# Neighbourhood attention of one layer in blocks of grid columns: 256 grid keys a block, scores in six one-bank places of PSUM

## The reference, cut to what matters

```python
def _neighbourhood_attention(q, k, v, kc, vc, rpb, scale):
    rows = length // GRID_W                      # 512 // 64 = 8
    wr = min(NA_ROWS, rows)                      # 8
    col = jnp.arange(GRID_W, dtype=jnp.int32)
    col_start = jnp.clip(col - NA_COLS // 2, 0, GRID_W - NA_COLS)      # NA_COLS = 16
    col_idx = col_start[:, None] + jnp.arange(NA_COLS, dtype=jnp.int32)[None, :]
    col_bias = rpb[:, :, col_idx - col[:, None] + (NA_COLS - 1)].astype(jnp.float32)
    ...
        s_nb = jnp.einsum('bhqd,bhrqkd->bhqrk', q_row, k_win).astype(jnp.float32) * scale + bias[None]
        s_ctx = jnp.einsum('bhqd,bhcd->bhqc', q_row, kc).astype(jnp.float32) * scale
        p = jax.nn.softmax(jnp.concatenate([s_nb.reshape(b, h, GRID_W, n_nb), s_ctx], axis=-1), axis=-1)
        ...
        return (jnp.einsum('bhqrk,bhrqkd->bhqd', p_nb, v_win)
                + jnp.einsum('bhqc,bhcd->bhqd', p[..., n_nb:], vc))
```

## Time and profile before

| | |
|---|---|
| median of 3 runs | 3726.51 us (3724.79 to 3728.86) |
| span of the profiled execution | 3722.8 us |
| the profiled execution's own time | not listed apart from its span; the median stands 3.7 us above it |
| PE busy | 3442.9 us, 92% of the span |
| DVE, ACT, POOL busy | 2015.8, 1320.7, 418.9 us |
| granted TensorE clock, mean | 0.972 |
| instructions | 47620 |
| near stage, first near scores to first matmul of `w_out` | 2116.77 to 2239.20 us of the span |

### The profile page before, as it was taken

How to read it: one execution, slowest core, us unless ns; L and a number is a source line. 1 busy time by engine, 2 the same in 40 slices (tenths; PEclk the granted TensorE clock), 3 DMA queues, 4 the chain that set the end, 5 groups by cost and what they waited for, 6 DMA issues and landing times. The chain is left out here.

```text
span 3722.8 us, 47620 instructions
## 1 busy us (share of the span) xinstructions
PE 3442.9 (92%) x19041; PEld 2781.6 (75%) x19041; DVE 2015.8 (54%) x3218; ACT 1320.7 (35%) x2013; POOL 418.9 (11%) x355
## 2 busy tenths in 40 slices
PE   6997889999989878999999878999999889989998
PEld 5885678888878656787787547888888666668886
DVE  3555556635546555868623764564554455555344
ACT  4224433212223354323222563531221644544233
POOL 2002440000000040000001570000000013300000
PEclk8997999999999999999999999999999999999999
DMA  5440033434422103555421002244343121113332
GB/s 184 124 124 24 1 90 104 132 99 125 125 68 68 46 1 97 164 158 171 131 71 40 11 21 61 76 127 122 101 128 89 47 45 31 33 57 97 96 104 72
DMA packets 466714, 322.59 MB, mean 87 GB/s; under 512 B 51408, under 2 KB 439262, under 8 KB 466496
## 3 DMA queue, kind: packets, MB, share of 16 engines
q1 hardware_dynamic: 456864, 299.93, 26.9%
q0 software_dynamic: 9632, 19.62, 1.9%
HBM read 312.94 MB, written 4.55 MB: 85 GB/s over the span
## 5 line engine op out<-in xcount | busy, mean ns | idle before, releaser
L1018 PE MATMUL PS<-HH,SPH 128*128 128x512 f32 (+1 forms) x3424 | 1180.2, 358 | 77.8 <-ACT HH L1781 20.7
L1018 PE MATMUL PS<-HL,SPH 128*128 128x512 f32 (+1 forms) x3424 | 1136.6, 355 | 4.8 <-DVE HL L2324 4.8
L1018 PEld LDWEIGHTS PS<-HH,SPH 128*128 128x128 f32 x3424 | 655.4, 191 | 194.9 <-issue 67.6
L1018 PE MATMUL PS<-HH,SPL 128*128 128x512 f32 (+1 forms) x3424 | 744.0, 357 | 0.0
L1018 PEld LDWEIGHTS PS<-HL,SPH 128*128 128x128 f32 x3424 | 646.3, 191 | 94.9 <-DVE HL L2324 7.7
L2207 DVE TENSOR_TENSOR SPL<-RAW,SPH 128x1024 fp32r<-128x1024 f32 (+3 forms) x367 | 458.1, 1248 | 389.5 <-ACT SPH L1647 388.8
L1018 PEld LDWEIGHTS PS<-HH,SPL 128*128 128x128 f32 x3424 | 582.8, 191 | 96.2 <-issue 5.3
L1647 ACT ACTIVATE SPH<-RAW 128x1024 fp32r<-128x1024 f32 (+3 forms) x367 | 393.9, 1074 | 720.3 <-PE PS L1018 464.5
L1018 PE MATMUL PS<-MH,SPH 128*128 128x512 f32 (+1 forms) x1056 | 361.8, 356 | 4.0 <-ACT SPH L1647 4.0
L1018 PE MATMUL PS<-ML,SPH 128*128 128x512 f32 (+1 forms) x1056 | 359.6, 355 | 0.0
L2521 DVE SCALAR_TENSOR_TENSOR X<-PS,MOD,X 128x512 f32<-128x512 f32 (+1 forms) x144 | 95.3, 662 | 403.1 <-PE PS L1018 401.2
(11 more groups left out here) (343 smaller groups left out, 3530.0 us busy)
## 6 DMA issues: line engine op xcount, KB each, us to landing
MS<-in_mod_turned SPq DMA_DIRECT2D x144, 512.0 KB, 3.4
RAW<-in_l_w_up SPq DMA_DIRECT2D x88, 512.0 KB, 3.8
RAW<-in_w_gate SPq DMA_DIRECT2D x44, 512.0 KB, 4.6
RAW<-in_w_val SPq DMA_DIRECT2D x44, 512.0 KB, 4.5
RAW<-in_w_down SPq DMA_DIRECT2D x32, 704.0 KB, 5.8
RAW<-in_l_w_down SPq DMA_DIRECT2D x32, 704.0 KB, 5.6
RAW<-in_w_in SPq DMA_DIRECT2D x40, 512.0 KB, 4.9
MS<-in_w_mod SPq DMA_DIRECT2D x32, 512.0 KB, 4.6
```

The costliest lines, as they stand in the source:

```text
L1018: return pe.matmul(o, a, b, start=start, stop=stop)
```

## The change

- **Layout.** `w_in`'s tiles of neighbourhood queries, keys and values are written to SBUF by grid columns: queries in four blocks u of 8 rows by 16 columns (columns 8-23, 24-39, 40-55, and 0-7 with 56-63), keys and values in four blocks of 8 rows by 16 columns. A query block needs only two key blocks, 256 keys. ACT's copy of a tile becomes three instructions for queries, two for keys and values.
- **Near steps** have 256 grid keys and 256 context keys: `nj` is 4 in place of 6. So 4 matmuls of 256 columns for scores, 8 transposes in two rounds, and an "o" of 4 matmuls over 256 queries (context) and 8 over 128 (grid).
- **PSUM.** A near side takes 512 columns, one bank, so that the three tiles hold six; the wait is for the exp of the side that last used the place.
- **Maxima, exp.** The custom instruction handles 256 columns and writes back to PSUM, one exp of 512 columns reads PSUM, and the addition of two sums is gone.
- **POOL** multiplies 512 columns a side and no longer loads biases.
- **The bias table** is half as large: 4 fills and 109 transfers of 1 to 16 columns. `load_bias` is 32 transfers of 16 partitions x 4 x 128, on SP's queue, all four pairs between the loads of `w_out`'s second and third tile.
- **Output.** The high and the low part of a near "o" are two instructions of 128 columns each, back in row order.

```diff
+NEAR = 256
...
-        BIAS = [[place(f"BIAS{r}{i}", [P, 14 * 64], F32, at0 + i * 3584) for i in range(2)]
+        BIAS = [[place(f"BIAS{r}{i}", [P, 4 * NEAR], F32, at0 + i * 16 * NEAR) for i in range(2)]
                 for r, at0 in enumerate((e0, big0 + 2 * TOK * 4))]
...
-        biasd = nc.dram_tensor("bias_rows", (64, 120 * 64), F32, kind="Internal").ap()
+        biasd = nc.dram_tensor("bias_rows", (64, 120 * 32), F32, kind="Internal").ap()
...
+        def query_cols(u):
+            return list(range(16 * u + 8, 16 * u + 24)) if u < 3 else [*range(8), *range(56, 64)]
+        def grid_block(x, u):
+            g = x.rearrange("p (r c) -> p r c", c=GRID_W)
+            if u < 3:
+                return g[:, :, 16 * u + 8:16 * u + 24]
+            return g.rearrange("p r (g k) -> p r g k", k=8)[:, :, 0:8:7, :]
+        def by_columns(x, c):
+            if 6 <= c < 10:
+                inner = x[:, 0:LAT].rearrange("p (r c) -> p r c", c=GRID_W)[:, :, 8:56]
+                return [(slice(0, 384), inner.rearrange("p r (u c) -> p u r c", u=3)),
+                        (slice(384, LAT), grid_block(x[:, 0:LAT], 3)), (slice(LAT, TOK), x[:, LAT:TOK])]
+            return [(slice(0, LAT), x[:, 0:LAT].rearrange("p (r u c) -> p u r c", u=4, c=16)), (slice(LAT, TOK), x[:, LAT:TOK])]
+        def near_keys(x, u):
+            if u < 3:
+                return x[:, P * u:P * u + NEAR]
+            return x.rearrange("p (b n) -> p b n", n=P)[:, 0:4:3, :]
+        def near_values(u, k):
+            return u + k if u < 3 else 3 * k
...
+            def place(self, n, e):
+                k = 2 * n + e
+                near = self.steps[n][0]["kind"] == "near"
+                return k % 3, 512 * (k // 3 % 2) if near else 0, 512 if near or self.steps[n][0]["nq"] < LAT else TOK
+            def place_free(self, n, e):
+                bank, a, m = self.place(n, e)
+                for k in range(2 * n + e - 1, -1, -1):
+                    other, b, w = self.place(k // 2, k % 2)
+                    if other == bank and b < a + m and a < b + w:
+                        return self.side(k // 2, k % 2) + 1
+                return self.sides_begin() if self.base["steps"] else 0
...
+            def out_parts(self, n, x, c):
+                G, blocks = self.steps[n]
+                if G["kind"] == "near":
+                    return [(slice(P * (u % 2), P * (u % 2) + P), grid_block(x[:, c, 0:LAT], u)) for u in (blocks[-1] - 1, blocks[-1])]
+                return [(slice(0, 256), x[:, c, self.out_cols(n)])]
...
+            def load_bias(p):
+                slots = biasd.rearrange("(u i) (b r n) -> i u b (r n)", u=4, b=2, n=16)
+                for e in range(2):
+                    for r in range(8):
+                        r0 = (2 * p + e) * 15 + 7 - r
+                        dst = BIAS[p % 2][e][16 * r:16 * r + 16, :].rearrange("p (u b n) -> p u b n", u=4, b=2)
+                        for b in range(2):
+                            sp.dma_start(dst[:, :, b, :], slots[:, :, b, r0 * 16:r0 * 16 + P]).then_inc(S.bias_landed[p % 2], 16)
+            def load_biases(A):
+                sp.wait_ge(S.bias_made, 16 * 109)
+                load_bias(0)
+                near = [n for n, (G, _) in enumerate(A.steps) if G["kind"] == "near"]
+                sp.wait_ge(S.s_done, A.side(near[0], 1) + 1)
+                load_bias(1)
+                for p in (2, 3):
+                    sp.wait_ge(S.bias_free, 8 * (p - 1))
+                    load_bias(p)
...
+                        if x is L["w_out"] and li == 2 and j == 2:
+                            load_biases(L["attention"])
...
-            def load_bias(p):
-                for e in range(2):
-                    for half in range(2):
-                        r0 = (2 * p + e) * 15 + (1 - half)
-                        pool.dma_start(BIAS[p % 2][e][64 * half:64 * half + 64, :], biasd[:, r0 * 64:(r0 + 14) * 64])\
-                            .then_inc(S.bias_landed[p % 2], 16)
...
-                    if G["kind"] == "near" and blocks == [0] and G["pair"] < 3:
-                        if G["pair"]:
-                            pool.wait_ge(S.bias_free, 8 * G["pair"])
-                        load_bias(G["pair"] + 1)
...
-                for k in range(8):
+                for k in range(4):
                     pool.dma_start(biasd.rearrange("c (a n) -> (c a) n", a=2)[:, k * 480:(k + 1) * 480], MASK[:]).then_inc(S.bias_filled, 16)
-                pool.wait_ge(S.bias_filled, 128)
+                pool.wait_ge(S.bias_filled, 64)
                 rpb = d["l0_rpb_2"].rearrange("h r c -> (h r) c")
-                flat = biasd.rearrange("c (r k) -> c r k", k=64)
-                for c in range(64):
+                flat = biasd.rearrange("c (b r k) -> c b r k", b=2, k=16)
+                for row in range(64):
+                    u, c = row // 16, query_cols(row // 16)[row % 16]
                     start = min(max(c - 8, 0), 48)
-                    pool.dma_start(flat[c, :, start:start + 16], rpb[:, start - c + 15:start - c + 31]).then_inc(S.bias_made, 16)
+                    split = 16 - start % 16
+                    block = start // 16 - u if u < 3 else start // 48
+                    for b, a, n, k in ((block, 16 - split, split, 0), (block + 1, 0, 16 - split, split)):
+                        if n:
+                            pool.dma_start(flat[row, b, :, a:a + n], rpb[:, start - c + 15 + k:start - c + 15 + k + n],
+                                           allow_slow_non_contiguous=n == 1).then_inc(S.bias_made, 16)
...
-                    ring = 2 if A.mla else 3
                     at = G["q0"] + blocks[0] * P
                     for e in range(2):
-                        if part == 0 and A.side(n, e) >= ring:
-                            pe.wait_ge(S.exp_done, A.side(n, e) - ring + 1)
...
+                            k, p0, _ = A.place(n, e)
+                            ps = PS[k]
                             nk = G["nj"] * P
-                            if nk == TOK:
+                            if G["kind"] == "near":
+                                a = NEAR * part
+                                keys = kt[rows, LAT:TOK] if part else near_keys(kt[rows, 0:LAT], blocks[0])
+                                last = mm(ps[:, p0 + a:p0 + a + NEAR], qt[rows, at:at + P], keys, True, True)
...
+                        for j in (2, 3):
+                            for e, rows in enumerate(G["rows"]):
+                                mm(turn_bank(r)[rows, 0:256], G["v"][e](LAT // P + j - 2), PTR[:, NTC * e + j, at:at + 256], j == 2, False)
+                        for u in (blocks[-1] - 1, blocks[-1]):
+                            a = P * (u % 2)
+                            for j in range(2):
+                                for e, rows in enumerate(G["rows"]):
+                                    last = mm(turn_bank(r)[rows, a:a + P], G["v"][e](near_values(u, j)), PTR[:, NTC * e + j, at + a:at + a + P],
+                                              False, j == 1 and u == blocks[-1])
+                        last.then_inc(S.t_done, 1)
+                        return
...
-                        if G["kind"] == "near":
-                            act.activation(ex[:, 0:LAT], ex[:, 0:LAT], ACT.Exp, bias=top, accum_out=total)
-                            last = act.activation(ex[:, LAT:TOK], ps[:, LAT:TOK], ACT.Exp, bias=top, accum_out=ctx_sum(n, e))
-                        else:
-                            last = act.activation(ex, ps, ACT.Exp, bias=top, accum_out=total)
+                        last = act.activation(ex, ps, ACT.Exp, bias=top, accum_out=total)
...
+                        if c < 6:
+                            act.activation(big(c), LIN[s % 2][:, 0:TOK], ACT.Copy).then_inc(S.tile_free, w.one(S.tile_free, t + 1))
+                        else:
+                            dst = VRAW[:, c - 14, :] if c >= 14 else big(c)
+                            for cols, src in by_columns(LIN[s % 2][:, 0:TOK], c):
+                                last = act.activation(shaped(dst[:, cols], src), src, ACT.Copy, scale=0.125 if 10 <= c < 14 else 1.0)
...
-                            if A.slot_turned(n, e):
-                                dve.wait_ge(S.t_done, A.slot_turned(n, e))
-                            ex, ps = A.probs(n, e), A.scores(n, e)
-                            b = BIAS[G["pair"] % 2][e][:, (6 - 2 * u) * 64:(6 - 2 * u) * 64 + LAT]
+                            ps = A.scores(n, e)
+                            b = BIAS[G["pair"] % 2][e][:, NEAR * u:NEAR * u + NEAR]
                             ctx_top, all_top = ATT[:, 32 + e:33 + e], ATT[:, 34 + e:35 + e]
-                            dve.tensor_reduce(ctx_top, ps[:, LAT:TOK], AX.X, ALU.max).then_inc(S.dve_step, w.one(S.dve_step))
+                            dve.tensor_reduce(ctx_top, ps[:, NEAR:2 * NEAR], AX.X, ALU.max).then_inc(S.dve_step, w.one(S.dve_step))
                             dve.wait_ge(*w.last)
```

(6 more changed lines are left out.)

53 lines of the change are left out of this document (31 added, 22 removed).

## The result

The changed kernel took 3705.69 us, the median of 4 runs (3702.32 to 3708.89); the kernel before took 3727.36 beside them. The ratio is 0.9942, 95% interval 0.9928 to 0.9956, or 22 us less. Measured again with 5 runs (experiment e1) it was 3703.15 us and 0.9932 (0.9918 to 0.9946), 25 us less. Forecast were 3701.5 us and 25.0 less.

A forecast was written before the change was run, and what follows sets the result against it. The near stage was taken as bound by hand-overs between engines running fixed lists; 25.2 us saved there less 0.2 for `w_in`'s last copy, 25.0 off 3726.5, gave 3701.5 us, range 3694 to 3716.

The forecast's parts named there:

- The sum: Near stage: 4.1 us saved in the first pair, 6.6 in each of three, 1.3 at the end, 25.2 us in all.
- The five intervals: Between score matmuls of one pair in the near stage: 5.5, 2.2, 5.9, 4.8 and 2.6 us, sum 21.0, before 27.64.
- fifth interval: Context scores in a pair: PE's own 1.07 + 0.57 + 0.57 and 0.4 for POOL or an exp, 2.6 us (4.47 before).
- last copy of `w_in`: ACT's copy before the first scores becomes three instructions: 0.2 us more, bounds 0.1 and 0.5.
- POOL's list for the table: 109 transfers for 64 and 4 fills less: about 24 us more issuing, no term, as POOL then idles until 1087.
- wait for exp: PE's 0.96 us wait in the second interval goes, as the place three sides back is another bank.
- DVE's lateness: Third interval: the "o" waits about 1.0 us for its bank, giving back the saving; 5.9 us (5.92 before).
- Small pieces cost as much as large ones: Rival, chance 0.12: narrow matmuls, custom instruction, POOL and "o" parts keep large prices, 15 us back, 3716 us.
- The bias queue binds: Rivals on SP's bias issues: mildly, from 0.66 us an issue, 3720 us (0.06); hard, from 0.92, 3769 us (0.04).
- The fourth interval: With the context step's short "o" in a pair: 4.8 us (5.91 before), including 0.3 wait for the high part.
- shortens an engine that is not late: Said of ACT: one exp of 512 columns, below 0.72 us, in place of 1.17 us for two.
- sign of being wrong: Pairs over 23 us apart, a reduce waiting for the bias, or time moving outside of 2019 to 2240 us.

The follow-up runs named there:

- e3: Changed kernel with the six PSUM places undone, near sides in a three-tile ring again: 3705.78 us, ratio 0.9937; stage 97.95 us.
- e6: Changed kernel with the custom instruction writing to SBUF again, two exps and the addition of two sums: 3702.62 us; stage 99.01 us.
- e7: Changed kernel with the 8 grid matmuls of an "o" over 256 queries in place of 128: 3706.7 us, ratio 0.9944; stage 100.72 us.
- e4: Changed kernel with each bias transfer on SP's queue split in two, 64 issues a pair in place of 32: 3734.39 us, ratio 1.0017.
- e5: Changed kernel with the same 32 bias transfers a pair issued by POOL in place of SP: 3743.39 us, ratio 1.0045; stage 142.2 us.
- e10: Changed kernel with DVE and ACT lists reordered as in e8, but third-round copies between the maxima's two sides: 3697.49 us, ratio 0.9920.
- e8: Changed kernel with the same instructions in another order in the DVE and ACT lists of near steps: 3701.23 us, ratio 0.9936.
- e9: Changed kernel with POOL multiplying 768 columns a side again in pairs two to four: 3712.97 us, ratio 0.9969; stage 105.7 us.

## Why the prediction was right

**The sum.** Against 25.2 us less in the stage stand 25.6, against 97.2 us, 96.8; pairs of 23.16, 21.32, 20.92, 20.81 and an end of 10.57 against 23.6, 21.0 three times and 10.5 (where the last pair is cut is a choice; together they are 31.4 against 31.5). The five intervals, forecast and second pair: 5.5 and 5.52, 2.2 and 2.09, 5.9 and 5.89, 4.8 and 4.70, 2.6 and 3.12. Only the fifth is off, by half a microsecond; in the third pair it was 2.74. One reading is off without effect: the scores behind the second pair start at 2172.01 in the trace, not at 2172.14, so its fifth interval was 4.34 us before.

**The prices.** Custom instruction 0.48 forecast, 0.493 measured; both sides of the maxima 2.12 and 2.23; "o" 2.0 and 1.96; POOL 1.6 and 1.56; exp below 0.72 and 0.69; the two parts of an "o" 0.07 more each and 0.05 to 0.07 (high 0.43 to 0.45 from 0.38, low 0.47 from 0.41); last copy of `w_in` 0.2 and 0.13, SP's issue 0.5 and 0.47 us. POOL's list for the table cost nothing that shows: e1's rest is not to be told from the spread.

**What is saved and given back.** The prediction said that the wait for exp goes and that DVE's lateness takes its gain back at the "o" behind it. e3 shows just that, 1.29 against 1.10 us. The gain is therefore not the PSUM places (1.2 us of 25.6). e3, e6 and e7 together are 7.0 us, and POOL's 256 columns in three of the four pairs 6.0 (9.0 with the clock's part). What is left, some 12 to 13 us, the prediction puts down to a third fewer columns in scores, transposes and maxima and to the third round that is gone; the intervals fit that, but no run undoes these.

**The rivals.** *Small pieces cost as much as large ones* falls with e7 (0.85 us for the "o") and with 0.493 against 0.751 us for the custom instruction. The rule of the Trainium skill, page "VectorE: DVE Perf Modes", section on the TRN2 errata, that instructions which read SBUF pay a fixed latency each, agrees in kind: the two durations leave 0.235 us for no columns, a third of the large one. How much of it is that latency no run here shows. By its extreme the stage would have lost 21 us and not 25.6. The median alone could not have refuted it: 21 us less would be 3705.5 us, nearer to the 3705.69 measured than the forecast was; the stage and the 0.493 us do. *The bias queue binds* had the right mechanism, and the point where it binds fits: at 0.47 us an issue it is hidden, with two issues for each it makes the kernel slower than before (e4). The 2.0 us that the page "DMA: Bandwidth & Descriptors" of the Trainium skill gives each transfer stand in its section on transfers that GpSimd issues, not SP. In e5, where POOL issued them, they took 2.0 us from issue to landing in the middle, which agrees; on SP's queue it was 1.9. One starts every 0.47 us, so they overlap, as the prediction took it.

**What was wrong.** Two terms, both small. The fourth interval has 0.3 us of waiting for ACT's high part; in after the low part starts with the end of DVE's reciprocals, 0.09 us after the high part, so that wait is next to nothing. The maxima, 0.11 us longer than forecast, hide a part of it. The other is the fifth interval: 0.4 us for POOL or an exp were in fact both, 0.46 and 0.31 in the second pair. That the single exp "shortens an engine that is not late" stands up in e6. But the part that it belongs to is worth 1.1 us, by the additions that DVE no longer does.

**The median.** 3705.69 us, 4.2 above the forecast; 3703.15 in e1, 1.7 above. The stage gave 0.4 us more than its sum, so the difference lies in the rest, which varied by 19 us between profiles: that the median came as near as this is luck, the stage is not. The prediction called it a sign of being wrong if time moved outside of 2019 to 2240 us. It did (the first scores of attention start 2.2 us later in after), but in e3, the same program up to there, the stage begins when it does in before. One step of 1.3 us is traced to the clock. That the whole spread is the clock was not shown.

## What to carry to other kernels

Where engines hand work to one another in fixed lists, walk one period interval by interval with prices from rows, and name for each interval the engine that ends it: here that gave a stage of 97 us to 0.4. An idle engine has room only behind the work that others wait for (e5), and a wait removed is worth what remains after the next one (e3). A total that comes out as expected does not show the cause: e6 met its number with half of it from the clock and the rest from another engine. Look at the rows and at the stage's granted clock. Once the work is smaller, look at the order of each list again: the same instructions in another order gave 5 us more in the stage (e10), a fifth of the whole change.

## What the runs showed of the hardware

- The rest of the program varied by 19 us from profile to profile while the near stage, at a granted clock of 1.00, repeated within 0.01 us: 96.78 and 96.79. A difference of 1 us is to be read in the stage, not in the median of 5 runs, and only between stages of the same granted clock: it was below 1.00 in five of the thirteen, and cost 1.2 us in e6, 1.6 in e8 and 3.0 in e9.
- The clock fell behind a wait of PE of 2.08 us in e8 and one of 1.59 us in e6, and not each time: after 1.59 us the scores took 1.84 us in the second pair of e6 and 1.14 in the third.
- After the same 3.50 us of idle time the same matmul ran at the upper level of the clock, 2.4 GHz, in one kernel (0.66 us) and at the lower, 1.2 GHz, in the other (1.19 us).
- The custom instruction costs as much with its output in PSUM (0.493 us) as in SBUF (0.484); the read of its accumulator behind it takes 0.14 us in place of 0.08.
- Halving a transfer of 32 KB left its issue at 0.47 us on SP's queue; POOL issues the 32 KB ones every 0.505 us, and its list does nothing else meanwhile (16.16 us for 32 in e5).
